# Quarter products in three pairs instead of seven in the first layer, and weight sums sent as a paced chain

## The reference, cut to what matters

```python
def conv_gated_ffn(x, w_up, w_gate, conv_w, conv_b, w_down):
    u = x @ w_up                                   # 512x1024 by 1024x2816
    g = causal_dwconv(x @ w_gate, conv_w, conv_b)  # three taps along the tokens
    return (jax.nn.silu(g) * u) @ w_down           # 512x2816 by 2816x1024
```

## Time and profile before

| | us |
|---|---|
| Median of three runs | 1976.14 |
| The profiled execution's own time | 1977.28 |
| Its span | 1975.3 |
| TensorE busy with matmuls | 1771.6 (90%) |
| DVE busy | 1179.4 (60%) |
| ACT busy | 914.7 (46%) |
| On the chain that ended last: matmuls | 68% |
| On the chain that ended last: loads into `wraw` | 15% |

### The profile page before, as it was taken

How to read it: one execution, slowest core, us unless ns; L and a number is a source line. 1 busy time by engine, 2 the same in 40 slices (tenths; PEclk the granted TensorE clock), 3 DMA queues, 4 the chain that set the end, 5 groups by cost and what they waited for, 6 DMA issues and landing times.

```text
span 1975.3 us, 25036 instructions
## 1 busy us (share of the span) xinstructions
PE 1771.6 (90%) x10221; PEld 1490.1 (75%) x10221; DVE 1179.4 (60%) x1864; ACT 914.7 (46%) x1436; POOL 36.5 (2%) x43
## 2 busy tenths in 40 slices
PE   9796999523479999999999998899999999999999
PEld 7574898523478888977777898888889886678766
DVE  5456797321365433738787866665335887566674
ACT  6557764211244322646765544443324545443542
POOL 0000100000000000000001000000000000000000
PEclk9898999866789999999999998899999999999999
DMA  8999825799963233221112344432332332123121
GB/s 300 298 250 238 210 68 170 250 255 237 243 189 112 99 101 99 83 80 54 54 54 70 113 149 149 133 115 94 106 96 86 94 96 75 54 75 107 60 70 43
DMA packets 67953, 258.35 MB, mean 131 GB/s; under 512 B 7424, under 2 KB 7680, under 8 KB 61056
## 3 DMA queue, kind: packets, MB, share of 16 engines
q1 hardware_dynamic: 60704, 176.02, 27.6%
q0 software_dynamic: 7136, 80.74, 16.9%
HBM read 252.54 MB, written 82.84 MB: 170 GB/s over the span
## 4 chain that ended last, share of the span: by engine, by line
PE 69%; DMA 15%; DVE 9%; ACT 5%; issue 1%; SPq 0%; POOL 0%; ACTq 0%; DVEq 0%; POOLq 0%
PE bank L606 68%; DMA wraw<-in_wstream 10%; DMA wraw<-tw 5%; DVE wl L2149 3%; ACT wh L1425 2%; ACT tmp L1425 2%; DVE tmp L2137 1%; DVE tmp L2140 1%; DVE sqr L2140 1%; DVE HL L2149 0%; PE bank L1370 0%; ACT HH L1425 0%; DVE acc_q L2140 0%; ACT taps L1425 0%; DVE X L2137 0%
## 5 line engine op out<-in xcount | busy, mean ns | idle before, releaser
L2149 DVE TENSOR_TENSOR wl<-wraw,wh 128x1024 fp32r<-128x1024 f32 (+1 forms) x306 | 370.1, 1219 | 445.5 <-ACT wh L1425 444.7
L1425 ACT ACTIVATE wh<-wraw 128x1024 fp32r<-128x1024 f32 (+1 forms) x306 | 319.4, 1052 | 497.0 <-PE bank L606 267.6
L606 PE MATMUL bank<-XH,wh 128*128 128x512 f32 (+1 forms) x1392 | 507.7, 365 | 8.9 <-DVE wl L2149 6.4
L606 PE MATMUL bank<-XL,wh 128*128 128x512 f32 (+1 forms) x1392 | 497.3, 358 | 0.0
L606 PE MATMUL bank<-XH,wl 128*128 128x512 f32 (+1 forms) x1392 | 496.8, 357 | 0.0
L606 PE MATMUL bank<-HL,wh 128*128 128x256 f32 (+1 forms) x868 | 255.6, 345 | 145.3 <-DVE acc_q L2140 79.3
L606 PEld LDWEIGHTS bank<-XH,wh 128*128 128x128 f32 x1392 | 265.9, 191 | 57.2 <-issue 10.8
L606 PEld LDWEIGHTS bank<-XH,wl 128*128 128x128 f32 x1392 | 265.7, 191 | 38.3
L606 PEld LDWEIGHTS bank<-XL,wh 128*128 128x128 f32 x1392 | 266.2, 191 | 35.2 <-issue 0.7
L606 PEld LDWEIGHTS bank<-HL,wh 128*128 128x128 f32 x868 | 163.6, 210 | 162.0 <-DVE acc_q L2140 80.0
L606 PE MATMUL bank<-HH,wh 128*128 128x256 f32 (+1 forms) x868 | 254.4, 344 | 6.6 <-DVE sqr L2140 3.3
(11 more groups left out here) (376 smaller groups left out, 2468.5 us busy)
## 6 DMA issues: line engine op xcount, KB each, us to landing
wraw<-in_wstream SPq DMA_DIRECT2D x248, 512.0 KB, 3.6
tw<-in_w POOLq DMA_DIRECT2D x22, 3584.0 KB, 36.0
wraw<-tw SPq DMA_DIRECT2D x112, 256.0 KB, 3.5
wraw<-in_wstream SPq DMA_DIRECT2D x30, 256.0 KB, 3.0
out<-X SPq DMA_DIRECT2D x8, 256.0 KB, 2.1
X<-in_xt SPq DMA_DIRECT2D x3, 512.0 KB, 8.4
pts<-in_pt SPq DMA_DIRECT2D x4, 256.0 KB, 4.1
eb<-lab SPq DMA_DIRECT2D x16, 64.0 KB, 2.0
```

The lines of the kernel that those rows point to most:

```text
L606: return pe.e.matmul(o, l, r, start=start, stop=stop, skip_group_check=True)
L1425: return act.e.activation(o, i, f, **kw)
L2149: return dve.e.tensor_tensor(o, x, h.bitcast(F32), ALU.subtract)
```

## The change

The number of pairs gets a value for each layer: three in the first, seven in the second. The eight column blocks of the first layer that leave the pairs are done as plain ones. The weight sums come in four parts, `SUMMED`: (layer, first and last tile, value of `w_lo` at which it starts, step). Each part is a chain of eight transfers, each of which waits for the one ahead of it to land and for `w_lo` to be one step further: copy T3, add, copy T2 from T3, add, copy T4 from T2, add, copy T1, add. Seven copies and adds of a quarter of all tiles become four copies and four adds of fewer tiles.

```diff
-PAIRS = 7
+PAIRS = (3, 7)
+
+SUMMED = [(0, 0, 4, 16, 1), (0, 4, 6, 38, 1), (1, 0, 6, 60, 4), (1, 6, 14, 100, 5)]
...
-    for p in range(PAIRS):
+    for p in range(PAIRS[layer]):
...
-                sp.wait_ge(s.tw, 176 * (layer + 1))
-                src = a["tw"][k // 4, layer, p + PAIRS * (mat[1] == "g")]
+                sp.wait_ge(s.tw, 128 * (summed_in(layer, 2 * p + (mat[1] == "g")) + 1))
+                src = a["tw"][k // 4, layer, 2 * p + (mat[1] == "g")]
...
-        for f in range(2 * PAIRS, FT):
+        for f in range(2 * PAIRS[layer], FT):
...
-    def weight_sums(layer):
-
-        t1, t3, t4, t2 = (a["tw"][t, layer].rearrange("n p c -> (n p) c") for t in range(4))
-        w11, w12, w21, w22 = (a[n][layer].rearrange("n p c -> (n p) c") for n in ("w11", "w12", "w21", "w22"))
-        pool.wait_ge(s.w_lo, (6, 60)[layer])
-        for t in (t1, t3, t2, t4):
-            pool.e.dma_start(t, w12).then_inc(s.tw, 16)
-        pool.wait_ge(s.tw, 176 * layer + 64)
-        for t, x in ((t1, w11), (t3, w22), (t2, w22), (t4, w22)):
-            pool.e.dma_start(t, x, accum_op=ALU.add, max_dma_last_dim=8192).then_inc(s.tw, 16)
-        pool.wait_ge(s.tw, 176 * layer + 128)
-        for t in (t2, t4):
-            pool.e.dma_start(t, w11, accum_op=ALU.add, max_dma_last_dim=8192).then_inc(s.tw, 16)
-        pool.wait_ge(s.tw, 176 * layer + 160)
-        pool.e.dma_start(t4, w21, accum_op=ALU.add, max_dma_last_dim=8192).then_inc(s.tw, 16)
+    def copy(dst, src, after):
+        pool.wait_ge(s.tw, 16 * after)
+        pool.e.dma_start(dst, src).then_inc(s.tw, 16)
+
+    def add(dst, src, after):
+        pool.wait_ge(s.tw, 16 * after)
+        pool.e.dma_start(dst, src, accum_op=ALU.add, max_dma_last_dim=8192).then_inc(s.tw, 16)
+
+    def weight_sums(part):
+
+        layer, n0, n1, at, step = SUMMED[part]
+        t1, t3, t4, t2 = (a["tw"][t, layer, n0:n1].rearrange("n p c -> (n p) c") for t in range(4))
+        w11, w12, w21, w22 = (a[n][layer, n0:n1].rearrange("n p c -> (n p) c") for n in ("w11", "w12", "w21", "w22"))
+        done = 8 * part
+        for n, (put, dst, src) in enumerate(((copy, t3, w12), (add, t3, w22), (copy, t2, t3), (add, t2, w11),
+                                             (copy, t4, t2), (add, t4, w21), (copy, t1, w12), (add, t1, w11))):
+            pool.wait_ge(s.w_lo, at + step * n)
+            put(dst, src, done + n)
 
     for i in (1, 3):
-        weight_sums(i // 2)
+        for part in ((0,), (1, 2, 3))[i // 2]:
+            weight_sums(part)
```

More of the change, by code:

```diff
@@ L51, in ffn_order @@
         out += [(up, k, f + 1) for k in range(4, KD)] + [(tg, k, p) for k in range(16)]
-    f = 2 * PAIRS
+    f = 2 * PAIRS[layer]
     out += [(f"up{layer}", k, f) for k in range(KD)] + [(f"gate{layer}", k, f - 1) for k in range(4, KD)]
     out += [(f"gate{layer}", k, f) for k in range(KD)]
-    for f in range(2 * PAIRS + 1, FT):
+    for f in range(2 * PAIRS[layer] + 1, FT):
         out += [(f"up{layer}", k, f) for k in range(KD)] + [(f"gate{layer}", k, f) for k in range(KD)]
@@ L242, in half_at, with pairs_before, summed_in @@
     return sum(TAIL[j] + SPLIT[j] for j in range(1, i) if PARTS[j] == 2 and j != 3)
+def pairs_before(layer):
+    return sum(PAIRS[:layer])
 def sums_of_pair(p):
     return [(p, 0, 1)] + [(p - 1, 1, 5)] * (p > 0) + [(p, 0, 2), (p, 0, 3), (p, 0, 4), (p, 1, 1), (p, 0, 5), (p, 1, 2), (p, 1, 3), (p, 1, 4)]
-SUMS = [x for p in range(PAIRS) for x in sums_of_pair(p)] + [(PAIRS - 1, 1, 5)]
+SUMS = [[x for p in range(n) for x in sums_of_pair(p)] + [(n - 1, 1, 5)] for n in PAIRS]
 def combined(layer, p, mat, j):
-    return 10 * PAIRS * layer + SUMS.index((p, mat, j)) + 1
+    return 10 * pairs_before(layer) + SUMS[layer].index((p, mat, j)) + 1
+def summed_in(layer, n):
+    return [q for q, (at, n0, n1, *_) in enumerate(SUMMED) if at == layer and n0 <= n < n1][0]
 def normed(i, f):
@@ L781, in first_products @@
             if p:
-                pe.wait_ge(s.u_e, 4 * (PAIRS * layer + p - 1) + 2 * g + 2)
+                pe.wait_ge(s.u_e, 4 * (pairs_before(layer) + p - 1) + 2 * g + 2)
             else:
@@ L825, in ffn @@
                 block(f"up{layer}", k, f, bu[:, :], XH[:, k, :], XL[:, k, :], k == 0, k == KD - 1)
-            if f == 2 * PAIRS:
-                last_product(1, PAIRS - 1)
-            if f >= 2 * PAIRS + 3:
+            if f == 2 * PAIRS[layer]:
+                last_product(1, PAIRS[layer] - 1)
+            if f >= 2 * PAIRS[layer] + 3:
                 pe.wait_ge(s.f_conv, FT * layer + f - 2)
@@ L1575, in ffn @@
             second_out(1, tg, p)
-        for f in range(2 * PAIRS, FT):
+        for f in range(2 * PAIRS[layer], FT):
             feed_group(up, range(KD), [f])
-            if f == 2 * PAIRS:
-                pair_gated(PAIRS - 1, 0)
+            if f == 2 * PAIRS[layer]:
+                pair_gated(PAIRS[layer] - 1, 0)
                 feed_group(gate, range(4, KD), [f - 1])
-                pair_gated(PAIRS - 1, 1)
+                pair_gated(PAIRS[layer] - 1, 1)
             feed_group(gate, range(KD), [f])
@@ L2343, in first_combined @@
             b, (o, _) = bank[3 * g:3 * g + 3], (sqr, m.gb)[g]
[L2344 removed]
+            dve.wait_ge(s.u_e, 4 * (pairs_before(layer) + p) + 2 * g + 1)
             tt(o[:, lo], o[:, lo], b[0][:, hi], ALU.add).then_inc(s.u_c, 1)
@@ L2378, in ffn @@
             three_combined(1, p)
-        for f in range(2 * PAIRS, FT):
+        for f in range(2 * PAIRS[layer], FT):
             feed_group(up, range(KD), [f])
-            if f == 2 * PAIRS:
+            if f == 2 * PAIRS[layer]:
                 gated(f - 2, sqr[0], m.gb[0])
                 feed_group(gate, range(4, KD), [f - 1])
-                last_combined(1, PAIRS - 1)
+                last_combined(1, PAIRS[layer] - 1)
                 gated(f - 1, sqr[1], m.gb[1])
```

22 lines of the change are left out of this document (11 added, 11 removed).

## The result

| | before | after |
|---|---|---|
| Median, us | 1976.94 (4 runs, 1974.38 to 1981.3) | 1792.65 (4 runs, 1789.88 to 1795.55) |
| Ratio | | 0.9066, 95% interval 0.9042 to 0.909 |
| Profiled execution, us | 1977.28 | 1790.65 |
| Its span, us | 1975.3 | 1788.9 |

The kernel is 184 us faster; 1795 was predicted, in a range of 1781 to 1822. First the page of the kernel after: sections 2 (forty slices, now of 44.7 us each), 3 and 4 (the chain that ended last, by engine).

A forecast was written before the change was run, and what follows sets the result against it. Weight sums holding the DMA engines were taken to set the time in the convolution and first layer's pairs, TensorE elsewhere. 135.8 + 40.2 + 4.9 = 180.9 us off 1977.3 gives 1796.4, 1795 as median; range 1781 to 1822.

The forecast's parts named there:

- Term 1: First layer's pairs: three pairs and plain blocks cut the stretch from 278.9 to 143.1 us, a gain of 135.8 us.
- Its price of a pair: First layer: a pair costs 27.2 us against 21.8 for two plain blocks, part of the gain, 20.3 us.
- Term 2: Convolution: periods stay at 16.1 us without the old copies, so dw(6) starts at 126.4, a gain of 40.2 us.
- the further gain that the text named: Convolution's end: dw(7)'s chain through ACT and DVE, 10.9 us behind dw(6), could give at most 6 us more; not counted.
- Term 3: pw2: ACT's wait for a unit held by the last add goes away, a gain of 4.9 us.
- The length of a step: POOL's chain, scaled by bytes: 3.4 and 6.5 us for 1024 KB copies and adds, 1.7 and 3.3 for 512 KB.
- POOL's steps are shorter than 7 us in the first part: Sign that the forecast holds: each transfer of the first part's chain takes under 7 us.
- The parts count for nothing: Later parts, under pairs, plain blocks, `down` and attention: no loss counted, 0 to 10 us held.
- ACT's waits in such places: Sign that the forecast is wrong: ACT's waits for `wraw` remain in `pg0` or the plain blocks.
- Columns, not waits: Rival, first layer's pairs: columns price a pair at 19.0 us, so removing four costs 11 us; 1826 us, chance 2%.
- The first part takes the place of the old sums: Rival, convolution: the first part slows the stream, 21 us lost, 1816 us, or 1805 to 1825; chance 17%.
- The chain is late: Rival, SP's wait for the second part: at 36.0 us a step the launch takes 2011 us, slower than before; chance 2%.

The follow-up runs named there:

- grouped: Kernel after with its four parts and starts, each done as the kernel before does: four copies at once, four adds, two, one; 1830.72 us.
- late_gated_7_7: Kernel after with seven pairs in both layers, no weight sums, and the odd block's gating behind the next pair's first recombinations; 1748.74 us.

## Why the prediction was right, point by point

- **What bounds the kernel: right.** Without any sums the old pair counts give 1810.67 us, so the sums' traffic was 166 us of the kernel before. The forecast's three terms hold 115.4 + 40.2 + 4.9 = 160.5 us of it.
- **Term 1, the first layer's pairs, 135.8 us: measured 138.2.** The three lengths it was made of came out as 26.0, 27.7 and 10.88 us. Its price of a pair (20.3 us for four) was measured alone at 21.3. Its place was right too, the wait at a pair's end and the low clock. What the text did not see is that this wait needs a pair behind the pair: the last pair of a layer doesn't pay it. With seven to three that changes nothing, since four joins go in any case; with three to none it does, and there a forecast from the same price missed by 14 us.
- **Term 2, the convolution, 40.2 us: measured 46.1 to dw(7).** dw(6) was 1 us off, and that is the start (dw(0) is at 28.44 in place of 29.73), so no period was lost. dw(7) follows it by 6.1 us instead of 10.9: the further gain that the text named, at most 6 us, and left out of the sum.
- **Term 3, 4.9 us: measured 4.0.**
- **The length of a step: mis-sized, at no cost.** The prediction scaled by bytes: 3.4 us for a copy and 6.5 for an add of 1024 KB, 1.7 and 3.3 for 512 KB. Measured were 5.0 to 8.3 and 10.1 to 11.7, then 3.8 to 4.7 and 7.9 to 9.6. A step has a fixed part that scaling from 3584 KB can't show. Against the limit of 9.1 us a step the mean of the second part was (283 - 225.7) / 8 = 7.2 us by issue times and the last landing: on time, with 15 us to spare in place of the 53 expected. The first part ended at 156.5 us and not near 140, still 23 us ahead of its norm's first sum on POOL (179.82). That steps of nearly three times the expected length (7.2 us for a mean of 2.5) did not reach the sum is owed to that room, not to the pricing. "POOL's steps are shorter than 7 us in the first part", a sign that the text named, was wrong. By the Trainium skill, page "DMA: Bandwidth & Descriptors", section "Anatomy of one DMA", a 512 KB transfer was estimated at 3.2 us; the copies took 3.8 to 4.7. It has no price for an accumulating one, which took 7.9 to 9.6.
- **The parts count for nothing: right, and now measured**, 3.3 us for all four together. ACT still waits 33.8 us in all for units of the stream (21 times, 4.4 at most) and 16.3 for the sums' tiles (5 times, 7.2 at most). Of this 16.7 us lie between 241 and 270 us, beside the second part, the longest (7.2) while TensorE is still in `pg0`, and 7.0 between 313 and 323, ahead of the first plain block. ACT's waits in such places were named as a sign of being wrong, and the sign misled: from 225 to 340 us TensorE waits only for `sqr`, twice, 8.7 us in all, so these waits cost nothing.
- **The rivals.** "Columns, not waits" was given 1826 us. It is false of a row of pairs, and for one pair alone its sign is true (1.2 us). "The first part takes the place of the old sums" is what grouped shows in small, 13.4 us. "The chain is late" did not occur; its text set the old transfers at 7 to 14 times the bytes of a step, where against the second part's 512 KB it is 7 times. The errors by stretch (+5.9, +2.4, -0.9, -1.9) sum to 5.5 us, the distance between the 180.9 us of the forecast and the 186.4 of the spans; between the medians it is 2.3 us.

## What to carry to other kernels

When side traffic starves a stream, move fewer bytes of it, in smaller parts, one transfer in flight at a time, so that the stream's lead covers each: beside three pairs in the first layer smaller and later parts were worth 54 us here, the chain in place of groups 38 (3.6 of it the pace, the rest not divided between number in flight and bytes), and after both the traffic was nearly free. When a count of something is cut and pays, ask whether its price belongs to the thing or to the seam between two: here undoing pairs and reordering one gating step out of the seam reach nearly the same time (1745.92 and 1749.39 us), and it took the run with no pair at all and the reordering to tell them apart. And an idle of 4.4 us of TensorE costs more than itself, since the clock is low behind it: 3.0 us of the idle and 2.1 us of slower matmuls went with each join.

## What the runs showed of the hardware that was not expected

- A transfer within HBM has a large fixed part beside a running stream. Accumulating ones of 512, 1024, 1536 and 2048 KB took 7.9, 10.6, 12.6 and 15.5 us at the median, copies of the first three sizes 3.8 to 4.7, 5.0 to 8.3 and 7.2 to 7.5. Lines through these, an estimate, are 5.4 us and 5.1 us for each 1024 KB for the accumulating ones, 2.6 us and 3.2 us for each 1024 KB for the copies.
- A 512 KB load on another queue takes 3.6 us alone, 3.4 to 11.2 beside one such transfer (medians of 4.4 and 5.2 over two stretches), 11 at the median beside up to four of 1 to 1.5 MB, and 45.7 in the one case beside four of 3.5 MB.
- 256-column matmuls of float32r stand 0.120 us apart at the upper clock and 0.213 at the lower, where 512 columns take 0.227 (10.88 / 48). Half the columns is a little more than half the time, so that 168 of them are 20.2 us and 96 full ones 21.8: 7% for the whole scheme, which one 4.4 us wait takes away. With the join mended a pair in a row of pairs still takes 22.2 us (late_gated_7_7), so the 7% does not arrive there either: TensorE still waits some 1.2 us for `acc_q` at each join (13.5 us in 11 waits).
